# One encoder layer with a product-key expert network: tile 0 goes first through all stages and is gathered; 320 tokens in the dense expert pass, V stationary

## What is computed

```python
h = rms_norm(x); q, k, v, u_g, v_g = split(h @ w_in)          # w_in 2048 x 5120
y_sb = stick_breaking_attention(norm(q), norm(k), v)            # 8 heads, causal, over all 512 tokens
y_sg = gelu(u_g) * (masked w_s per block of 128 @ norm(gelu(v_g)) + b_s)
x = x + concat(rms_norm(y_sb), rms_norm(y_sg)) @ w_out          # 2048 x 2048
h2 = rms_norm(x)
q = rms_norm(h2 @ w_query)                                      # 8 heads x 2 x 128
s1, s2 = q[.., 0] @ keys[0].T, q[.., 1] @ keys[1].T             # 128 keys each
# per head the 16 best of the 16 x 16 sums of the best s1 and s2: 128 experts of 16384 per token
act = gelu(expert_u[idx] . h2) * softmax(top_scores)
x = x + sum over the 128 experts of act * expert_v[idx]
```

## Time and profile before

| what | value |
|---|---|
| median of three runs (lowest to highest) | 3323.76 us (3322.66 to 3328.01) |
| the profiled execution: its span, first to last instruction | 3322.0 us |
| PE busy | 3181.5 us, 96% |
| DVE busy | 2225.3 us, 67% |
| POOL busy | 1107.3 us, 33% |
| ACT busy | 1016.0 us, 31% |
| moved by DMA | 703.63 MB, mean 212 GB/s |

### The profile page before, as it was taken

The page is one execution under the profiler, slowest core; times in us unless marked ns, Lnnn a source line. Parts: engine busy times, 40 slices in busy tenths (PEclk is TensorE's granted clock), DMA queues, the critical chain, the costliest instruction groups (busy, mean ns, idle before and its releaser), DMA issues.

```text
span 3322.0 us, 44218 instructions
## 1 busy us (share of the span) xinstructions
PE 3181.5 (96%) x16025; PEld 2826.3 (85%) x16025; DVE 2225.3 (67%) x3201; ACT 1016.0 (31%) x1027; POOL 1107.3 (33%) x1122
## 2 busy tenths in 40 slices
PE   6999987899999988999989999999999999999997
PEld 6888865687889988999978888889999999999996
DVE  2222233322224999787649999998888888888884
ACT  3222227523222322333323223222222222222221
POOL 0000000000003544443431111166666666666660
PEclk9999998899999999999999999999999999999999
DMA  3222220222222433565689999988888888888884
GB/s 130 100 101 88 101 88 0 77 99 78 89 89 101 142 123 100 169 193 184 186 288 307 302 307 305 307 316 343 324 332 331 329 323 333 327 331 324 334 332 140
DMA packets 279552, 703.63 MB, mean 212 GB/s; under 512 B 13168, under 2 KB 152480, under 8 KB 219840
## 3 DMA queue, kind: packets, MB, share of 16 engines
q1 hardware_dynamic: 166288, 390.10, 33.7%
q0 software_dynamic: 38064, 274.90, 21.3%
q10 hardware_dynamic: 75136, 37.75, 4.0%
HBM read 660.76 MB, written 41.94 MB: 212 GB/s over the span
## 4 chain that ended last, share of the span: by engine, by line
PE 84%; DVE 10%; ACT 2%; issue 2%; DMA 1%; POOL 0%; DVEq 0%; SPq 0%; ACTq 0%; POOLq 0%; PEldq 0%
PE ps L1092 26%; PE ps L1094 26%; PE ps L1093 26%; PE ps L1298 3%; PE ps L1104 1%; DVE eq L954 1%; DVE i12u L922 1%; PE ps L1181 1%; DVE eq L952 1%; DVE tpos L922 1%; DVE v L920 1%; DVE ring_lo L744 1%; DVE tv L920 1%; PE ps L1195 1%; DVE sel L955 1%
## 5 line engine op out<-in xcount | busy, mean ns | idle before, releaser
L475 ACT ACTIVATE ring_hi<-ring_raw 128x2048 fp32r<-128x2048 f32 x328 | 628.4, 1916 | 1161.8 <-PE ps L1094 1153.4
L744 DVE TENSOR_TENSOR ring_lo<-ring_raw,ring_hi 128x2048 fp32r<-128x2048 f32 x263 | 602.2, 2290 | 434.9 <-ACT ring_hi L475 428.8
L1092 PE MATMUL ps<-actT_hi,ring_hi 128*128 128x384 f32 (+1 forms) x2304 | 790.5, 343 | 5.8 <-DVE ring_lo L744 2.3
L1094 PE MATMUL ps<-actT_hi,ring_lo 128*128 128x384 f32 (+1 forms) x2304 | 787.2, 342 | 0.0
L1093 PE MATMUL ps<-actT_lo,ring_hi 128*128 128x384 f32 (+1 forms) x2304 | 786.9, 342 | 0.0
L1092 PE MATMUL ps<-ring_hi,a_hi 128*128 128x512 f32 x1536 | 601.9, 392 | 23.5 <-DVE ring_lo L744 13.2
L1093 PE MATMUL ps<-ring_lo,a_hi 128*128 128x512 f32 x1536 | 602.1, 392 | 0.0
L1094 PE MATMUL ps<-ring_hi,a_lo 128*128 128x512 f32 x1536 | 601.9, 392 | 0.0
L425 POOL TENSOR_TENSOR ring_lo<-ring_raw,ring_hi 128x2048 fp32r<-128x2048 f32 x65 | 304.7, 4688 | 775.5 <-ACT ring_hi L475 775.5
L441 POOL TENSOR_TENSOR small<-small 128x1 f32<-128x1 f32 x512 | 306.7, 599 | 721.4 <-DVE x L1037 354.8
L1092 PEld LDWEIGHTS ps<-actT_hi,ring_hi 128*128 128x128 f32 x2304 | 435.1, 189 | 20.0 <-DVE ring_lo L744 3.1
(11 more groups left out here) (154 smaller groups left out, 2874.2 us busy)
## 6 DMA issues: line engine op xcount, KB each, us to landing
ring_raw<-peer_u SPq DMA_DIRECT2D x128, 1024.0 KB
ring_raw<-peer_v SPq DMA_DIRECT2D x128, 1024.0 KB
ring_raw<-w_in SPq DMA_DIRECT2D x40, 1024.0 KB
gates_scratch<-gbuf ACTq DMA_DIRECT2D x24, 1024.0 KB, 6.7
free_lo<-gates_scratch SPq DMA_DIRECT2D x64, 384.0 KB
ring_raw<-w_out SPq DMA_DIRECT2D x16, 1024.0 KB
ring_raw<-w_query SPq DMA_DIRECT2D x16, 1024.0 KB
gelu_scratch<-free_hi ACTq DMA_DIRECT2D x64, 192.0 KB, 2.9
```

The costliest lines, as they stand in the source:

```text
L475: act.activation(hi[:, slot, :], raw[:, slot, :], ACT.Copy).then_inc(hi_made, 1)
L744: dve.tensor_tensor(lo[:, slot, :], raw[:, slot, :], hi[:, slot, :].bitcast(F32), ALU.subtract)\
L1092: pe.matmul(dst, w_h, m_h, start=first, stop=False)
L1094: return pe.matmul(dst, w_l, m_h, start=False, stop=last)
```

## The change

Four things change together, and with them the order of nearly all instructions.

1. **Tile 0 goes first.** Its input projection (40 pieces of 12 matmuls), attention, gating, output and query run alone on its 128 tokens, with pieces of the other three tiles put between. So `w_in`, `w_out` and `w_query` are read twice: 72 more pieces. Tile 0 takes the place of the far tile, is retrieved while the others are in their input projection, and its rows are gathered from there on.
2. **64 more tokens are gathered**, the last 64 of the sequence. A gather of 128 rows serves two choices of each, so there are 64 + 64 more. The dense pass has `NEAR` = 320 tokens.
3. **V is stationary** in the down pass: 48 matmuls a piece that move 320 columns; the sum comes out with tokens as columns, DVE adds it to `yT` (`add_y`), and at the end PE turns it back. V's pieces are laid out so that a partition reads 8 KB in one run.
4. **Order and room.** The ring has four slots (three for the pieces from `IN_B2` to `AHEAD`), and `ring_lo` takes the place of `ring_raw`. 96 up pieces go ahead instead of 64; then 92 down pieces and 32 pairs. POOL makes `ring_lo` for 252 pieces (14 in the input projection, all ahead and down, three in four of the both stage, two of the last four) instead of 65. Weighted rows are summed in four banks of PSUM (`acc`) instead of in SBUF. The number of rows at each piece is in a table, `ROWS_AT`: 103 before the first up piece, 83 while ahead, 123 in down, 77 in both, 386 in all with two that switch `acc` over. The small POOL operations ahead of a gather are gone.

```diff
-NEAR = SEQ - P
-PRE = 64
-RING_SLOTS = 2
+NB = SEQ - P
+G2 = 64
+NEAR = NB - G2
+PRE = 96
+IN_A, IN_B0, OUT_A, IN_B1, QUERY_A, IN_B2, OUT_B, QUERY_B, AHEAD = 0, 40, 44, 60, 62, 78, 112, 128, 144
+DOWN = AHEAD + PRE
+BOTH = DOWN + GROUP * (PRE_GROUPS - 1)
+LAST = BOTH + 2 * GROUP * (N_GROUPS - PRE_GROUPS)
...
+SLOT = [n % 4 if n < IN_B2 else (n - IN_B2) % 3 if n < AHEAD else (n - AHEAD) % 4 for n in range(N_PIECES)]
+POOL_A = range(IN_B2, 92)
+def lo_on_pool(n):
+    if n in POOL_A or AHEAD <= n < BOTH:
+        return True
+    if n < BOTH:
+        return False
+    if n < LAST:
+        return (n - BOTH) % 2 == 0 or (n - BOTH) // 2 % 2 == 0
+    return (n - LAST) % 2 == 0
...
+AHEAD_TILE = 12
+HOT_FIRST = 3 * AHEAD_TILE + 1
+RETRIEVE_ROWS = (4, 8, 12, 16, 20)
+for _i in range(6 * BATCHES):
+    HOT_AT[HOT_FIRST + _i] = 1 if _i % 6 == 5 else 3
...
+            def one_row(r):
...
+                dve.wait_ge(gathered[b], ROW_FULL[r])
+                if kind == "u" or kind == "u2":
...
+                    dve.tensor_tensor_reduce(out=src, in0=src, in1=h_far[:] if kind == "u" else acc, scale=1.0,
+                                             scalar=0.0, op0=ALU.mult, op1=ALU.add, accum_out=z[:, s:s + 1])\
+                       .then_inc(row_used, 1)
+                elif kind == "v" or kind == "v2":
...
+                        dve.scalar_tensor_tensor(out=acc, in0=src, scalar=a[:, s:s + 1], in1=acc, op0=ALU.mult,
+                                                 op1=ALU.add).then_inc(row_used, 1)
...
+            for i in range(GROUP, PRE):
+                v = i - GROUP
+                n = DOWN + v
+                if v:
+                    add_y(v - 1, 3)
+                rows_step(1 if ROWS_AT[n] else 0)
+                add_y(v, 0)
+                gate_down(i)
+                add_y(v, 1)
+                rows_step(ROWS_AT[n] - (1 if ROWS_AT[n] else 0))
+                add_y(v, 2)
...
+            def piece_a(n, kq, bank):
+                s = place(n)
+                pe.wait_ge(lo_ok[SLOT[n]], USE[n])
+                for kk in range(4):
+                    k = 4 * kq + kk
+                    cols = slice(kk * BANK, (kk + 1) * BANK)
+                    for w, m, first, end in ((aT_hi, ring_hi, k == 0, False), (aT_hi, ring_lo, False, False),
+                                             (aT_lo, ring_hi, False, k == KD - 1)):
+                        last = pe.matmul(ps[:, bank, :], w[:, k, :], m[s][:, cols], start=first, stop=end)
...
+                    for kk in range(4):
+                        k = 4 * kq + kk
+                        for w, m in ((ring_hi, aT_hi), (ring_hi, aT_lo), (ring_lo, aT_hi)):
+                            for b in range(4):
+                                first = k == 0 and b == 0 and w is ring_hi and m is aT_hi
+                                last = pe.matmul(ps[:, 1 + c % 2, b * P:(b + 1) * P],
+                                                 w[s][:, kk * BANK + b * P:kk * BANK + (b + 1) * P], m[:, k, :],
+                                                 start=first, stop=True, skip_group_check=True)
...
+            def down(s, use, v4, c, par, own=None):
...
+                for j in range(4):
+                    if j == 3 and own is not None:
+                        pe.wait_ge(alo_made, own)
+                    else:
+                        pe.wait_ge(y_added, v4 + ((j + 1) % 4 + 1))
+                    dst = ps[:, (c + 1 + j) % 4, 0:NEAR]
+                    for e in range(GROUP):
+                        col = slice(e * BANK + j * P, e * BANK + (j + 1) * P)
+                        pe.matmul(dst, hi[:, col], a_hi[:, par, e, :], start=(e == 0), stop=False)
+                        pe.matmul(dst, hi[:, col], a_lo[:, par, e, :], start=False, stop=False)
+                        last = pe.matmul(dst, lo[:, col], a_hi[:, par, e, :], start=False, stop=(e == GROUP - 1))
```

2217 lines of the change are left out of this document (1332 added, 885 removed).

## The result

The changed kernel takes **3410.16 us** (median of four runs, 3385.85 to 3433.0) against 3323.45 before: a ratio of **1.0257**, 95% interval 1.0217 to 1.0297. It is slower; the prediction was 3130 us, in a range of 3065 to 3245. The four runs fall into two pairs, 3386 and 3390 at a mean granted clock of 0.95, 3431 and 3433 at 0.94. Each ratio in this document is taken from a kernel's fast runs alone, so it can lie off the quotient of the two medians.

A forecast was written before the change was run, and what follows sets the result against it. It took TensorE, busy 3181.5 of 3322.0 us, as the bound. Stage times along the new kernel's path summed to a span of 3125 us; with 2 us around it, 3127, stated as 3130 us, range 3065 to 3245.

The forecast's parts named there:

- TensorE's price of a matmul: Dense stretches: a matmul costs its columns at 2.4 GHz plus 13.3 ns, so 146.7 ns for 320 columns.
- rival 4: Up and down: 320-column matmuls go no faster than 384-column ones, 173.3 ns; +327 us, 3457 us; 5%.
- the last stage: Both: 32 pairs of up and down pieces at 14.08 us, 451 us, then the end of the kernel.
- Rival 5: Down and both: weighted rows summed in PSUM also hold the port; +313 and +87 us, 3530 us; 2%.
- Query of tile 0: 16 x 48 matmuls of 128 columns at 117 ns, 90 us, plus 8 for the scores.
- Rival 1: Query of tile 0: narrow split matmuls run as four passes, 227 ns each; +84 us, 3214 us; 12%.
- Attention: Gating and attention of the other three tiles with turning: 150 us, 12 gathered rows included; 160.5 us before.
- The other tiles' input: Input projection of the other tiles: 34 pieces at 8.16 us, 277 us, gathered rows beside PE-bound pieces.
- One-hot pieces: Up pieces with one-hot work after the retrievals: 11.5 us with three quads, 8 with one; 335 us in all.
- rival 2: Down and one-hot: the port sets the pace; 8.2 us a down piece, +74, one-hot +17, 3221 us; 12%.
- Down: 92 down pieces at GpSimd's 7.4 us, above TensorE's 7.04 and VectorE's 6.5: 681 us.
- Input of tile 0: 40 pieces of 12 matmuls at 3.0 us through four slots, 120 us, plus 40 for work in between.

The follow-up runs named there:

- e1_att0: The changed kernel without the 12 gathered rows in the attention stage, done in the last stage instead; 3361.99 us, ratio 1.0128 to before.
- e13_norows: The changed kernel without gathered rows in the other tiles' input and the 30 one-hot pieces, done later; input 281 us instead of 304, one-hot pieces 348.6 instead of 393.3.
- e14_accgate: The changed kernel with VectorE's one-hot and down gate operations reading their first operand from the accumulator in PSUM, wrong values; 3235.82 us, one run.
- e8_short: The changed kernel with GpSimd subtracting only 64 of 2048 columns in down, the product with V's rest left out; 3292.96 us, one run.

## Why the prediction was wrong, point by point

- **Right.** TensorE's price of a matmul, N/2.4 ns + 13.3: 147 ns for 320 columns, which also sends rival 4 (173 ns) off. (It does not reach down to 128 columns: 67 ns by it, 111 measured. For those the row of plain fp32 was taken, rightly.) The start at 18 us, the out projection, the 36 ups with the retrievals (258 for 257), the last stage (499 for 500). Rival 5 too: the sums in PSUM take 2344 ns and are never stretched. The widths gave the 258 us they were to give; of these 65 were to go into longer gaps, and 365 did, a clock at half rate included (the span grew by 107).
- **Query of tile 0, +44 in half of the runs.** The price of 98 us was right when the clock holds, with some luck: in e1_att0 the matmuls and scores take 91, and 6 more go by until the next piece is ready. I had no term for a clock that halves while TensorE is fully busy. Rival 1 (four passes, 227 ns) is not what happened: at full clock the pitch is 111 ns.
- **Attention, +43.** The step was "12 gathered rows are put in: 150". I counted the rows as free; they stand between two links of the chain VectorE, TensorE, ScalarE, and e1_att0 takes 147 us without them.
- **The other tiles' input, +27.** "34 pieces x 8.16" had VectorE's share counted but not the wait for a gather with two row buffers, 60.9 us in 24 waits; e13_norows takes 281.
- **One-hot pieces, +65 of the +75.** Two terms. The price of a three-quad piece was 11.5, measured 12.8 on the mean of the 21 that open no later batch (10.8 and 13.5 to 15 in turn): 27. The term in it that was too small is "about 3.8 blocked": above their medians, hot_a and hot_b take 113 us in these pieces, 4.5 for each of the 25 with three quads, the full block of rival 2 (12.3). And a term was missing: gbuf is one buffer, 4 MB, so the four pieces that open a second to fifth batch take 21.2 on the mean instead of 11.5: 39. The other 10 us of the 75 are in the plain ups and the changeover.
- **Down, +97.** The step that failed is VectorE's 6.5 us a piece. It has the two gate operations at about 0.5 each and nothing for the port, and the reason for that nothing is the one given against rival 2: "ScalarE's split, which releases GpSimd, follows the gate, so they should fall into step". They don't; the gate operations are blocked 1.05 and 0.71 us on the mean (1527 - 482, 1204 - 492). That makes VectorE's 6.5 us 8.3, above TensorE's 7.04 and near the 8.45 measured, and TensorE waits 84.6 us for the sums behind them. Rival 2, at 12%, had the mechanism and nearly the price (8.2 for 8.45). I also took GpSimd's sum, 7.4, for the bound. Without the port the stage takes 680 us, my 681, whether GpSimd works or not: that figure was right by chance, and what holds there is the DMA engines at a share of 0.96 or TensorE at 7.04.
- **Input of tile 0, +10.** The 160 us from the first piece on (120 for the ring, 40 counted from the order of instructions) were 170. Which of the two was short was not tried; open.
- **The two rules weighed.** The Trainium skill's page "SBUF — State Buffer", section "SBUF: two separate sides", calls the pair of ports an exclusive lock. The trace agrees in e14_accgate, with 482 against 1527 ns. I had this rule and the row that bears it out before me, wrote that they speak against moving 252 subtractions to GpSimd, and gave rival 2, which they stand behind, 12%. The 358 GB/s that the Trainium skill's same page gives in the section "A bandwidth-pool intuition that's wrong" were not the limit: e8_short moves 378 GB/s for 678 us.

The range failed mainly in down, in the one-hot pieces, in attention and in the other tiles' input, each a matter of VectorE's order, and I let its share (6.5 of 7.04 us a piece) stand as enough room. The halved clock and the single gate buffer are misses of another kind. The chance of rival 2 should have been the largest.

## What to carry to other kernels

An engine that is busy 87% of a stage, as VectorE in down, and stands in TensorE's chain can be the bound already: price what it waits for under each of its operations, not only its own durations. An elementwise pass that is moved to GpSimd can hold up those operations of VectorE that have their operands in SBUF and meet it in time. Look for those in the chain first, or give them an operand in PSUM. Work put in "for free" has a place in an order, and what is behind it in that place pays.
